# Two transformer blocks on one core: six weight chunks of the first block rounded and split by GpSimd, eight short vectors loaded later or not at all

## The chip, the cores and the metric

The kernel runs on one core of one Trainium2 chip. The metric is the device time of one launch in microseconds. The engines of the core are named as in the profile: PE (TensorE matmuls), PEld (its weight loads), DVE (VectorE), ACT (ScalarE), POOL (GpSimd) and SP (SyncE, which here only issues DMAs).

## The reference, cut to what matters

Two blocks run one after the other on 256 tokens of width 1024, in float32, each with two layers. The change touches the first block only, whose layer is:

```python
def hybrid_layer(x, c, positions, ...):
    mod = jax.nn.silu(c) @ w_ada + b_ada
    shift, scale, gate = jnp.split(mod[:, None, :], 3, axis=-1)
    h = rms_norm(x, norm_g) * (1 + scale) + shift
    z = h @ w_in
    c_q, c_kv, k_rope, g_mla, q_b, k_b, v_b, g_moba = jnp.split(z, list(IN_OFFSETS), axis=-1)
    o_mla = mla_attention(c_q, c_kv, k_rope, positions, mla_q_norm_g, mla_w_uq,
                          mla_kv_norm_g, mla_w_ukv, mla_q_g, mla_k_g)
    o_moba = moba_attention(q_b, k_b, v_b, moba_q_g, moba_k_g, rel_bias)
    y = jnp.concatenate([jax.nn.silu(g_mla) * o_mla, jax.nn.silu(g_moba) * o_moba], axis=-1) @ w_out
    return x + gate * y
```

With 256 tokens the "moba" attention is one causal block with a bias by distance. Its 8 heads have width 64; the "mla" attention has 8 heads of 96, whose last 32 columns are rotated. The second block (two SwiGLU feed-forwards around three attentions) needs four lambda vectors, a norm's gain and the sinks, the "short vectors" of the change.

## The kernel before

**Products.** Every matrix product keeps nearly full float32 accuracy with three passes. A weight chunk (128 partitions x 1024 or 512 columns) is loaded by SP into one of 6 buffers `raw`. ACT rounds it to fp32r into one of 5 buffers `wh` (line 903, signal `hi`), DVE subtracts to get the rest into `wl` (line 1513, signal `lo`), and PE multiplies x_h by wh, x_h by wl and x_l by wh (line 472). A chunk of 1024 columns gives PE 12 matmuls. ACT works up to four chunks ahead of PE and DVE three (class `Stream`, `take` and `split`), in a place of each engine's own program that is fixed when the kernel is built. A `wh` buffer is written again when PE has done the chunk five before it; SP issues the load of chunk c when chunk c - 6 has both `hi` and `lo`.

**Other loads in the same buffers.** The rows of `w_ada` also pass through `raw`. DVE adds each, weighed by silu(c), to a row (`weigh`; the profile names it by where the row lies: `acc`, `qt`, `qkv`, always `SCALAR_TENSOR_TENSOR x<-raw,st,x`).

**Order of a layer of the first block, `l` = 0 and 1.** PE runs the gemms z, qb, kb, vb (the last three give `qkv`), then turns the normed queries and keys (`turn_heads`, line 476), then the gemms q0, q1, kv0, kv1 (4 chunks: 1024, 512, 512 and 512 columns) and gmla (4 chunks of 1024). The moba attention runs as side steps between these gemms. One step k is: PE scores (`pb<-kt,qt`), DVE adds the bias and takes the maximum (line 1516), ACT takes the exponential (`pb<-pb,st`), PE turns the result, ACT copies it (`pt<-pb`), PE multiplies by v (`pb<-qkv,pt`). There are eight scores, k0 to k7. In the four steps of gmla the function `prep` is mixed in: ACT squares the mla queries (`th<-mq`), DVE sums them (line 2023), POOL takes the power -0.5 (`rstd`, line 2422), DVE waits for it before its next line-1516 operation. The evictions `qkv`, `mq`, `mkv` and the copies `qt`, `kt` are ACT's.

**POOL** has little work: the `rstd` of 1 or 8 columns, DMAs of broadcast rows, and 16 additions `G<-G,mg` of 512 columns in the second block (line 2504). After the `rstd` of qb of layer 0 it issues `vectors()` (line 2438): ten DMAs that broadcast short rows over all partitions into `bc`, 1424 columns in all.

Of the kernel before, what the change touches and what calls it, by code (L numbers as in the profile page):

```python
# [8 lines left out]
F = mybir.dt.float32  # L9
# [11 lines left out]
NRAW = 6  # L21
# [229 lines left out]
def build(nc, d, out, ctx):  # L251
# [16 lines left out]
    cols = sb("cols", [128, 128])  # L268
    bc = sb("bc", [128, 1440])
    st = sb("st", [128, NSTAT])  # L270
# [87 lines left out]
    bc_of, bc_in, n_bc = {}, [], 0  # L358
    for name, n in (("mla_q_g", 96), ("mla_k_g", 96), ("moba_q_g", 64), ("moba_k_g", 64),
                    ("diff_lambda_q1_2", 64), ("diff_lambda_k1_2", 64), ("diff_lambda_q2_2", 64),  # L360
                    ("diff_lambda_k2_2", 64), ("diff_subln_g_2", 128), ("sw_sink_2", 8)):
        bc_of[name] = (n_bc, n)
        bc_in.append((name, n_bc, NL * n))
        n_bc += NL * n
# [99 lines left out]
    def pe(e):  # L464
# [33 lines left out]
        def gemm(g, x, k0, key, src, n0, n, by, head=1, tail=1, between=None, mid=None, roll=0, soon=None,  # L498
                 two_sides=False):
            wv = src.rearrange("(c p) n -> p c n", p=128)  # L500
# [5 lines left out]
            pair_no[0] += 1  # L506
            first_bank = 2 * ((pair_no[0] - 1) % 2)
            for gi, group in enumerate(groups(nk, n, head, tail)):
                taken = [take(wv[:, (c0 + roll) % nk:(c0 + roll) % nk + kk, :, wide] if two_sides else
                              wv[:, (c0 + roll) % nk:(c0 + roll) % nk + kk, wide], kk, n,  # L510
                              ("mm", g, 1) if c0 + kk == nk else None) for c0, kk in group]
                for t in range(2):
                    o = banks[first_bank + t][:, 0:n]
                    for (c0, kk), (c, hi, lo) in zip(group, taken):
                        for k in range(kk):
                            kx, final = k0 + c0 + k, c0 + k == nk - 1
                            xh, xl = (v[:, kx, t * 128:t * 128 + 128] for v in x)
                            if c0 + k == 0:
                                open_bank(first_bank + t, (by, g, t))
                            w.wait_ge(*at("xh", *key(t, kx)))  # L520
                            w.wait_ge(*at("hi", c))
                            mm(o, xh, hi[:, k, :], c0 + k == 0, False)
                            w.wait_ge(*at("lo", c))
                            mm(o, xh, lo[:, k, :], False, False)
                            w.wait_ge(*at("xl", *key(t, kx)))
                            last = mm(o, xl, hi[:, k, :], False, final)
                            if final:
                                last.then_inc(*up("mm", g, t))
                            elif t == 1 and k == kk - 1:
# [166 lines left out]
        for l in range(NL):  # L696
# [49 lines left out]
            gemm(("kv0", l), XC, 2, ckey, d["mla_w_ukv"][l], 0, 512, "eva")  # L746
            gemm(("kv1", l), XC, 2, ckey, d["mla_w_ukv"][l], 512, 512, "eva")
            side.mix((None for _ in range(6)), 6)
            side.over(4)
            gemm(("gmla", l), XT, 0, xkey, win, 416, 512, "evd")  # L750
            side.drain()
# [138 lines left out]
    def act(e):  # L890
# [17 lines left out]
        def split(chunks):  # L908

            for c in chunks:  # L910
                src, kk, n, _, i, ada_ = plan[c]
                if ada_:
                    continue
# [580 lines left out]
    def dve(e):  # L1494
# [27 lines left out]
        def split(chunks):  # L1522

            for c in chunks:
                src, kk, n, _, i, ada_ = plan[c]
                if ada_:
                    weigh(c)
                    continue
                w.wait_ge(*at("hi", c))
                if i >= NW:  # L1530
# [313 lines left out]
        for l in range(NL):  # L1844
# [173 lines left out]
            def prep():  # L2018
                for t in range(2):
# [6 lines left out]
                    qr = heads(mq[:, t, :], 96)[:, :, 64:96]  # L2026
                    w.wait_ge(*at("bc"))
                    w.wait_ge(*at("eva", ("q1", l), t))
# [384 lines left out]
    def pool(e):  # L2413
# [20 lines left out]

        def vectors():

            for name, a0, n in bc_in:
                e.dma_start(bc[:, a0:a0 + n], bass.AP(tensor=d[name].tensor, offset=0, ap=[[0, 128], [1, n]])).then_inc(
                    *landed("bc"))

# [7 lines left out]
        for l in range(NL):  # L2448
# [36 lines left out]
        for l in range(NL):  # L2485
            for kind in ("f1", "mx", "f2"):
# [34 lines left out]
    def sp(e):  # L2521
        w = Waits(e)
        for c, (src, kk, n, _, _, _) in enumerate(plan):
            if c >= NRAW:
# [67 lines left out]
```

## Time and profile before

| | us |
|---|---|
| median of 3 runs | 1612.37 (1612.14 to 1613.6) |
| profiled execution, its own time | 1614.55 |
| its span, first to last instruction | 1612.7 |
| PE busy | 1561.8 |
| DVE, ACT, POOL busy | 1070.1, 872.2, 119.7 |
| mean granted TensorE clock | 0.992 of full speed |

PE is busy 97% of the span, so an engine other than PE matters only where PE waits for it or for what it delays. The stretches of the first attention are 80 to 132 us (layer 0) and 237 to 276 us (layer 1). Times on the left of a row are microseconds from the start of the span. A row of the waits or the timeline shows in brackets how long the engine stood idle before it, and what ended that.

### The profile page before, as it was taken

The page shows a single profiled execution, that of the slowest core. Times are in us where ns is not written, and L with a number is a line of the kernel's source. Part 1 is how long each engine was busy: PE and PEld are TensorE (multiplying, and loading weights), DVE is VectorE, ACT ScalarE, POOL GpSimd, SP SyncE. Part 2 cuts the span into 40 slices and gives each one's busy share as a digit, 9 for nine tenths or more (in the row PEclk, how much of TensorE's full clock was granted, in tenths as well). Part 3 has the DMA queues.
Part 4 walks back from the last instruction along what each step waited for, and adds up shares of the span by engine and source line. Part 5 has one row for each costly group of instructions (what it writes and reads, how often), then busy time and mean ns, then how long its engine had stood idle before and what let it go on. Part 6 is the DMA issues. An engine that isn't in the chain of part 4 may idle for free.

```text
span 1612.7 us, 21335 instructions
## 1 busy us (share of the span) xinstructions
PE 1561.8 (97%) x7540; PEld 1295.7 (80%) x7540; DVE 1070.1 (66%) x1779; ACT 872.2 (54%) x1526; POOL 119.7 (7%) x146
## 2 busy tenths in 40 slices
PE   5989999999999999999999999999999999999998
PEld 4768787788888888887788887888788888778886
DVE  7977877665555667687755647565666678676553
ACT  3676567554444656564644446444566656554442
POOL 0400021011000000021000001000000002100000
PEclk9999999999999999999999999999999999999999
DMA  9974473379855534546655557975553454665651
GB/s 341 303 252 157 161 253 122 101 183 220 212 183 169 183 93 137 176 144 209 195 183 183 190 189 190 194 205 195 170 183 112 143 158 145 202 207 171 200 185 73
DMA packets 149090, 293.16 MB, mean 182 GB/s; under 512 B 10128, under 2 KB 23216, under 8 KB 148984
## 3 DMA queue, kind: packets, MB, share of 16 engines
q1 hardware_dynamic: 143424, 276.60, 52.0%
q0 software_dynamic: 4416, 12.29, 6.9%
q10 hardware_dynamic: 1144, 2.92, 0.5%
q8 instruction: 60, 0.98, 0.2%
q14 instruction: 46, 0.38, 0.1%
HBM read 290.70 MB, written 1.06 MB: 181 GB/s over the span
## 4 chain that ended last, share of the span: by engine, by line
PE 86%; DVE 5%; ACT 4%; DMA 3%; issue 2%; POOL 1%; SPq 0%; DVEq 0%; POOLq 0%; ACTq 0%
PE pb L472 81%; PE pb L476 4%; DVE wl L1513 1%; DMA raw<-in_w_in 1%; DMA raw<-in_w_ada 1%; ACT wh L903 1%; DVE xt_l L1510 1%; DMA raw<-in_mla_w_ukv 1%; ACT pb L903 1%; DVE mkv L1510 1%; POOL st L2422 0%; DVE h L1510 0%; ACT xt_h L903 0%; ACT ti L903 0%; DVE st L2023 0%
## 5 line engine op out<-in xcount | busy, mean ns | idle before, releaser
L903 ACT ACTIVATE wh<-raw 128x1024 fp32r<-128x1024 f32 (+1 forms) x484 | 507.5, 1054 | 432.3 <-PE pb L472 408.0
L1513 DVE TENSOR_TENSOR wl<-raw,wh 128x1024 fp32r<-128x1024 f32 (+1 forms) x484 | 582.7, 1220 | 203.1 <-ACT wh L903 198.3
L472 PE MATMUL pb<-wh,xt_h 128*128 128x512 f32 (+2 forms) x1472 | 579.7, 394 | 5.4 <-issue 2.9
L472 PE MATMUL pb<-wh,xt_l 128*128 128x512 f32 (+2 forms) x1472 | 574.0, 390 | 2.8 <-DVE xt_l L1510 1.7
L472 PE MATMUL pb<-wl,xt_h 128*128 128x512 f32 (+2 forms) x1472 | 570.8, 388 | 0.0
L472 PEld LDWEIGHTS pb<-wh,xt_l 128*128 128x128 f32 x1472 | 277.8, 189 | 67.6 <-DVE xt_l L1510 10.2
L472 PEld LDWEIGHTS pb<-wh,xt_h 128*128 128x128 f32 x1472 | 278.3, 189 | 61.5 <-issue 7.2
L472 PEld LDWEIGHTS pb<-wl,xt_h 128*128 128x128 f32 x1472 | 278.4, 189 | 53.1
L472 PE MATMUL pb<-wh,big_h 128*128 128x512 f32 x352 | 137.8, 391 | 0.0
L472 PE MATMUL pb<-wh,big_l 128*128 128x512 f32 x352 | 137.1, 389 | 0.0
L472 PE MATMUL pb<-wl,big_h 128*128 128x512 f32 x352 | 136.9, 389 | 0.0
L2422 POOL TENSOR_TENSOR st<-st,cols 128x1 f32<-128x1 f32 (+2 forms) x56 | 54.7, 982 | 926.9 <-DVE st L1510 665.8
L472 PEld LDWEIGHTS pb<-wh,big_l 128*128 128x128 f32 x352 | 66.1, 188 | 13.9
L472 PEld LDWEIGHTS pb<-wl,big_h 128*128 128x128 f32 x352 | 66.1, 188 | 13.6
L472 PEld LDWEIGHTS pb<-wh,big_h 128*128 128x128 f32 x352 | 66.1, 188 | 13.4
L1510 DVE SCALAR_TENSOR_TENSOR sgt<-ti,pb 128x512 f32<-128x512 f32 (+1 forms) x48 | 30.7, 644 | 61.2 <-ACT ti L903 61.0
L1510 DVE SCALAR_TENSOR_TENSOR hid<-pb,few,sgt 128x512 f32<-128x512 f32 (+1 forms) x48 | 33.9, 706 | 47.2 <-PE pb L472 46.3
L903 ACT ACTIVATE p<-p,st 128x256 f32<-128x256 f32 x96 | 48.3, 504 | 29.4 <-DVE st L1516 29.4
L903 ACT ACTIVATE pt<-pb 128x512 f32<-128x512 f32 (+1 forms) x80 | 40.3, 504 | 26.3 <-PE pb L476 26.3
L903 ACT ACTIVATE big_h<-pb 128x512 fp32r<-128x512 f32 x44 | 24.2, 597 | 39.1 <-PE pb L476 39.1
L903 ACT ACTIVATE ti<-pb,few 128x512 f32<-128x512 f32 (+1 forms) x48 | 31.4, 657 | 20.8 <-PE pb L472 20.3
L2504 POOL TENSOR_TENSOR G<-G,mg 128x512 f32<-128x512 f32 x16 | 24.3, 1522 | 246.2 <-DVE mg L1510 245.8
(243 smaller groups left out, 1552.6 us busy)
## 6 DMA issues: line engine op xcount, KB each, us to landing
raw<-in_ffn_w_gu SPq DMA_DIRECT2D x160, 512.0 KB, 4.7
raw<-in_w_in SPq DMA_DIRECT2D x148, 512.0 KB, 4.2
raw<-in_ffn_w_down SPq DMA_DIRECT2D x88, 512.0 KB, 4.0
raw<-in_w_ada SPq DMA_DIRECT2D x48, 512.0 KB, 5.4
raw<-in_w_out SPq DMA_DIRECT2D x32, 512.0 KB, 4.2
raw<-in_w_branch SPq DMA_DIRECT2D x24, 512.0 KB, 4.0
raw<-in_ffn_w_gu SPq DMA_DIRECT2D x32, 256.0 KB, 4.9
raw<-in_w_in SPq DMA_DIRECT2D x8, 416.0 KB, 4.6
```

The costliest lines, as they stand in the source:

```text
L472: return e.matmul(o, a, b, start=start, stop=stop)
L476: return e.transpose(o, a, ident[0:n, 0:n])
L903: return e.activation(o, a, func, **kw)
L1510: return e.scalar_tensor_tensor(out=o, in0=a, scalar=s, in1=b, op0=op0, op1=op1)
L1513: return e.tensor_tensor(o, a, b, op)
L2422: e.tensor_tensor(stat(n, "rs", *name), v, halves.to_broadcast([128, n]) if n > 1 else halves, ALU.pow).then_inc(*up("rs", *name))
L2504: e.tensor_tensor(m, m, mg[mg_at(n, n0, t)][:, :], ALU.add).then_inc(*up("mrg", g, t))
```

## The change

- `gemm` gets an argument `pool`, a set of chunk numbers. In each layer chunk 0 of kv1 (512 columns) and chunks 1 and 3 of gmla (1024 columns each) are marked. ACT and DVE leave them out; POOL makes both parts in a new function `split`: `tensor_copy` for wh (signal `hip`), then `tensor_tensor` subtract for wl (`lop`). PE and SP wait for `hip` and `lop` where they waited for `hi` and `lo`.
- In POOL's program kv1's chunk and gmla's chunk 1 come before the `rstd` of the first half of the mla queries, gmla's chunk 3 between that and the next `rstd`.
- `vectors` at its old place issues only the two mla gains (384 columns, signal `bcm`). The two moba gains, read by nothing from `bc`, are dropped (256 columns). The six vectors of the second block (784 columns) are issued in the first feed-forward of the second block.

```diff
-            gemm(("kv1", l), XC, 2, ckey, d["mla_w_ukv"][l], 512, 512, "eva")
+            gemm(("kv1", l), XC, 2, ckey, d["mla_w_ukv"][l], 512, 512, "eva", pool=(0,))
...
-            gemm(("gmla", l), XT, 0, xkey, win, 416, 512, "evd")
+            gemm(("gmla", l), XT, 0, xkey, win, 416, 512, "evd", pool=(1, 3))
...
+        def split(g, *which):
+
+            for c0 in which:
+                c = pool_splits[g, c0]
+                kk, n, _, i, _ = plan[c][1:6]
+                hi, lo, v = (a[i % m][:, 0:kk * n] if m == NW else a[c % m][:, 0:kk * n]
+                             for a, m in ((wh, NW), (wl, NW), (raw, NRAW)))
+                w.wait_ge(*at(f"raw{c % NRAW}", c))
+                if i >= NW:
+                    w.wait_ge(*at(*plan[split_at[i - NW]][3]))
+                e.tensor_copy(hi, v).then_inc(*up("hip", c))
+                w.wait_ge(*at("hip", c))
+                e.tensor_tensor(lo, v, hi.bitcast(F), ALU.subtract).then_inc(*up("lop", c))
...
                 if l == 0 and nm == "qb":
-                    vectors()
-            for nm in ("mq", "mk"):
-                for t in range(2):
-                    rstd(8, nm, l, t)
+                    vectors(bc_in[:2], "bcm")
+            split(("kv1", l), 0)
+            split(("gmla", l), 1)
+            rstd(8, "mq", l, 0)
+            split(("gmla", l), 3)
+            for nm, t in (("mq", 1), ("mk", 0), ("mk", 1)):
+                rstd(8, nm, l, t)
...
                     if kind == "f1":
+                        if l == 0:
+                            vectors(bc_in[2:], "bc")
                         bias_table(s, l)
```

POOL in layer 0, from the power for qb on. Before:

```order
16 L2422 TENSOR_TENSOR st<-st,cols 128x8 [waits s_var] x2
17 L2438 DMA bc<-in_mla_q_g 128x192
18 L2438 DMA bc<-in_mla_k_g 128x192
19 L2438 DMA bc<-in_moba_q_g 128x128
20 L2438 DMA bc<-in_moba_k_g 128x128
21 L2438 DMA bc<-in_diff_lambda_q_2 128x128
22 L2438 DMA bc<-in_diff_lambda_k_2 128x128
...
25 L2438 DMA bc<-in_diff_subln_g 128x256
26 L2438 DMA bc<-in_sw_sink 128x16
27 L2422 TENSOR_TENSOR st<-st,cols 128x8 [waits s_var] x6
28 L2470 DMA mk<-in_b_ada 128x1024 [waits s_tr]
```

The same place after the change (`CAST` is the `tensor_copy`; 128x512 is kv1's chunk, the 128x1024 ones are gmla's):

```order
16 L2438 TENSOR_TENSOR st<-st,cols 128x8 [waits s_var] x2
17 L2454 DMA bc<-in_mla_q_g 128x192
18 L2454 DMA bc<-in_mla_k_g 128x192
19 L2438 TENSOR_TENSOR st<-st,cols 128x8 [waits s_var] x2
20 L2467 CAST wh<-raw 128x512 [waits s_w,s_raw3]
21 L2469 TENSOR_TENSOR wl<-raw,wh 128x512 [waits s_hip]
22 L2467 CAST wh<-raw 128x1024 [waits s_mm,s_raw1]
23 L2469 TENSOR_TENSOR wl<-raw,wh 128x1024 [waits s_hip]
24 L2438 TENSOR_TENSOR st<-st,cols 128x8 [waits s_var]
25 L2467 CAST wh<-raw 128x1024 [waits s_mm,s_raw0]
26 L2469 TENSOR_TENSOR wl<-raw,wh 128x1024 [waits s_hip]
27 L2438 TENSOR_TENSOR st<-st,cols 128x8 [waits s_var] x3
```

The eight other DMAs are gone from here, and the powers of the mla queries (rows 24 and the first of 27) now stand behind the splits.

ACT in layer 0, from the rounding of q0's chunk on. Before:

```order
68 L903 ACTIVATE wh<-raw 128x1024 [waits s_raw4]
69 L903 ACTIVATE wh<-raw 128x512 [waits s_w,s_raw0]
70 L903 ACTIVATE wh<-raw 128x512 [waits s_w,s_raw1]
71 L903 ACTIVATE wh<-raw 128x512 [waits s_w,s_raw3]
72 L903 ACTIVATE qkv<-pb 128x512 [waits s_mm] x2
73 L903 ACTIVATE qt<-pb 128x512 [waits s_tr] x2
```

After:

```order
68 L917 ACTIVATE wh<-raw 128x1024 [waits s_raw4]
69 L917 ACTIVATE wh<-raw 128x512 [waits s_w,s_raw0]
70 L917 ACTIVATE wh<-raw 128x512 [waits s_w,s_raw1]
71 L917 ACTIVATE qkv<-pb 128x512 [waits s_mm] x2
72 L917 ACTIVATE qt<-pb 128x512 [waits s_tr] x2
```

The rounding of kv1's chunk (row 71 before) no longer stands ahead of the evictions of vb and the copies `qt`.

DVE in layer 1, around the first score. Before:

```order
319 L1513 TENSOR_TENSOR wl<-raw,wh 128x512 [waits s_raw4,s_w,s_hi]
320 L1510 SCALAR_TENSOR_TENSOR acc<-raw,st,acc 128x1024 [waits s_acc,s_raw5]
321 L1513 TENSOR_TENSOR wl<-raw,wh 128x512 [waits s_raw0,s_w,s_hi]
322 L1516 ISA pb,st<-pb,mbias 128x128 [waits s_pt,s_sc]
...
326 L1513 TENSOR_TENSOR wl<-raw,wh 128x1024 [waits s_raw1,s_mm,s_hi]
327 L1510 SCALAR_TENSOR_TENSOR acc<-raw,st,acc 128x1024 [waits s_acc,s_raw2]
```

After:

```order
316 L1527 TENSOR_TENSOR wl<-raw,wh 128x512 [waits s_raw4,s_w,s_hi]
317 L1524 SCALAR_TENSOR_TENSOR acc<-raw,st,acc 128x1024 [waits s_acc,s_raw5]
318 L1530 ISA pb,st<-pb,mbias 128x128 [waits s_pt,s_sc]
...
322 L1527 TENSOR_TENSOR wl<-raw,wh 128x1024 [waits s_raw1,s_mm,s_hi]
323 L1524 SCALAR_TENSOR_TENSOR acc<-raw,st,acc 128x1024 [waits s_acc,s_raw2]
324 L1530 ISA pb,st<-pb,mbias 128x128 [waits s_pt,s_sc]
```

Only the subtraction of kv1's chunk (row 321 before) left this place; the split of gmla's chunk 0 (row 322 after) and a weighed row still stand between the first score and the second.

## Rows read from the trace of the kernel before

**Rows 1.** The page's chain that ended last, share of the span by engine.

```profile
PE 86%; DVE 5%; ACT 4%; DMA 3%; issue 2%; POOL 1%; SPq 0%; DVEq 0%; POOLq 0%; ACTq 0%
```

**Rows 2.** PE's waits from 60 to 335 us: total, times, longest.

```profile
PE pb L472 <- ACT pt L903: 5.2, 5, 1.5
PE pb L476 <- ACT qt L903: 3.8, 1, 3.8
```

**Rows 3.** Timeline of ACT, layer 0: start, duration, operation, [idle before].

```profile
85.16 0.63 ACT L903 ACTIVATE wh<-raw 128x512 fp32r<-128x512 f32 x1 [1.32 <-DMA raw<-in_mla_w_ukv]
85.69 1.07 ACT L903 ACTIVATE qkv<-pb 128x512 f32<-128x512 f32 x2
...
101.57 1.07 ACT L903 ACTIVATE wh<-raw 128x1024 fp32r<-128x1024 f32 x1
```

**Rows 4.** DMA from 70 to 80 us: queue, packets, MB, share of 16 engines.

```profile
q0 software_dynamic: 332, 0.66, 71.3%
q1 hardware_dynamic: 445, 0.73, 24.4%
```

**Rows 5.** Timeline of PE, layer 0.

```profile
82.92 0.55 PE L476 MATMUL pb<-cst,qkv 128*128 128x128 f32 x3 [0.21 <-DVE qkv L1513]
87.30 1.11 PE L476 MATMUL pb<-cst,qkv 128*128 128x128 f32 x4 [3.83 <-ACT qt L903]
88.07 0.77 PE L472 MATMUL pb<-wh,xc_h 128*128 128x512 f32 x1
...
122.25 1.97 PE L472 MATMUL pb<-qkv,pt 128*128 128x64 f32 x8 [1.50 <-ACT pt L903]
```

**Rows 6.** Timeline of DVE, layer 0, the end of the gemm vb.

```profile
78.78 2.28 DVE L1513 TENSOR_TENSOR mbias<-sg,cst 128x2048 f32<-128x2048 f32 x1
80.99 0.68 DVE L1513 TENSOR_TENSOR wl<-raw,wh 128x512 fp32r<-128x512 f32 x1
81.59 1.28 DVE L1513 TENSOR_TENSOR qkv<-qkv,st 128x512 f32<-128x512 f32 x2
```

**Rows 7.** Stretches of PE: us, PE busy, granted clock, DMA share, GB/s.

```profile
85.00:91.00 6.00, 3.70 (x11) 0.50 0.97 343
122.00:129.00 7.00, 6.75 (x20) 0.51 0.38 111
269.00:272.00 3.00, 3.00 (x10) 0.50 0.22 72
```

**Rows 8.** POOL's groups by shape: busy, mean ns of one | idle before.

```profile
L2504 POOL TENSOR_TENSOR G<-G,mg 128x512 f32<-128x512 f32 x16 | 24.3, 1522 | 246.2 <-DVE mg L1510 245.8
L2441 POOL MEMSET ones<- 128x128 f32 x1 | 0.2, 205 | 0.3 <-POOLq L2577 0.3
```

**Rows 9.** POOL and DVE from 738 to 743 us, single operations, ns min/median/max.

```profile
L2504 POOL TENSOR_TENSOR G<-G,mg x2: 1293/1747/2201, 738.7 to 740.1; 128x512 f32<-128x512 f32 x2
L1513 DVE TENSOR_TENSOR wl<-raw,wh x2: 1221/1768/2314, 739.9 to 741.1; 128x1024 fp32r<-128x1024 f32 x2
```

**Rows 10.** Timeline of DVE, layer 1, from the first score to the second.

```profile
241.25 1.22 DVE L1513 TENSOR_TENSOR wl<-raw,wh 128x1024 fp32r<-128x1024 f32 x1
242.39 1.28 DVE L1510 SCALAR_TENSOR_TENSOR acc<-raw,st,acc 128x1024 f32<-128x1024 f32 x1
243.58 0.28 DVE L1516 CUSTOM_DVE_ANT_0 pb<-pb,mbias 128x128 f32<-128x128 f32 x1
```

**Rows 11.** Timeline of PE, layer 1.

```profile
244.94 0.41 PE L476 MATMUL pb<-cst,pb 128*128 128x128 f32 x2 [0.19 <-ACT pb L903]
...
251.02 1.13 PE L472 MATMUL pb<-kt,qt 128*128 128x512 f32 x2 [1.21 <-ACT pt L903]
...
268.34 1.50 PE L472 MATMUL pb<-qkv,pt 128*128 128x64 f32 x8 [1.51 <-ACT pt L903]
```

**Rows 12.** The chain that ended last, layer 1: start, us, what.

```profile
256.44 1.75 POOL st L2422
...
262.59 1.75 POOL st L2422
```

**Rows 13.** Timeline of DVE, layer 1, between these two powers.

```profile
259.87 1.22 DVE L1513 TENSOR_TENSOR wl<-raw,wh 128x1024 fp32r<-128x1024 f32 x1
261.30 1.01 DVE L2023 TENSOR_REDUCE st<-th 128x4 f32<-128x384 f32 x2 [0.21 <-ACT th L903]
```

More of the change, by code:

```diff
@@ L268, in build @@
     cols = sb("cols", [128, 128])
-    bc = sb("bc", [128, 1440])
+    bc = sb("bc", [128, 1184])
     st = sb("st", [128, NSTAT])
@@ L358, in build @@
     bc_of, bc_in, n_bc = {}, [], 0
-    for name, n in (("mla_q_g", 96), ("mla_k_g", 96), ("moba_q_g", 64), ("moba_k_g", 64),
-                    ("diff_lambda_q1_2", 64), ("diff_lambda_k1_2", 64), ("diff_lambda_q2_2", 64),
+    for name, n in (("mla_q_g", 96), ("mla_k_g", 96), ("diff_lambda_q1_2", 64), ("diff_lambda_k1_2", 64), ("diff_lambda_q2_2", 64),
                     ("diff_lambda_k2_2", 64), ("diff_subln_g_2", 128), ("sw_sink_2", 8)):
@@ L395, in chunk_view, with upper, lower @@
         return buf[:, 0:kk * n].rearrange("p (k n) -> p k n", n=n)
+    pool_splits = {}
+    def upper(c):
+        return ("hip" if c in pool_splits.values() else "hi", c)
+    def lower(c):
+        return ("lop" if c in pool_splits.values() else "lo", c)
     def weighed(l, j, kx):
@@ L498, in gemm @@
         def gemm(g, x, k0, key, src, n0, n, by, head=1, tail=1, between=None, mid=None, roll=0, soon=None,
-                 two_sides=False):
+                 two_sides=False, pool=()):
             wv = src.rearrange("(c p) n -> p c n", p=128)
@@ L507, in gemm @@
             first_bank = 2 * ((pair_no[0] - 1) % 2)
+            n_chunk = 0
             for gi, group in enumerate(groups(nk, n, head, tail)):
+                for i in range(len(group)):
+                    if n_chunk in pool:
+                        pool_splits[g, n_chunk] = c_no[0] + i
+                    n_chunk += 1
                 taken = [take(wv[:, (c0 + roll) % nk:(c0 + roll) % nk + kk, :, wide] if two_sides else
@@ L520, in gemm @@
                             w.wait_ge(*at("xh", *key(t, kx)))
-                            w.wait_ge(*at("hi", c))
+                            w.wait_ge(*at(*upper(c)))
                             mm(o, xh, hi[:, k, :], c0 + k == 0, False)
-                            w.wait_ge(*at("lo", c))
+                            w.wait_ge(*at(*lower(c)))
                             mm(o, xh, lo[:, k, :], False, False)
@@ L911, in split @@
                 src, kk, n, _, i, ada_ = plan[c]
-                if ada_:
+                if ada_ or c in pool_splits.values():
                     continue
@@ L1528, in split @@
                     continue
+                if c in pool_splits.values():
+                    continue
                 w.wait_ge(*at("hi", c))
@@ L2026, in prep @@
                     qr = heads(mq[:, t, :], 96)[:, :, 64:96]
-                    w.wait_ge(*at("bc"))
+                    w.wait_ge(*at("bcm"))
                     w.wait_ge(*at("eva", ("q1", l), t))
@@ L2433, in bcast, with vectors @@
                         ).then_inc(*landed(f"ring{i}", *key))
-        def vectors():
-            for name, a0, n in bc_in:
+        def vectors(which, to):
+            for name, a0, n in which:
                 e.dma_start(bc[:, a0:a0 + n], bass.AP(tensor=d[name].tensor, offset=0, ap=[[0, 128], [1, n]])).then_inc(
-                    *landed("bc"))
+                    *landed(to))
+        def split(g, *which):
[10 more added lines that the diff above has]
+                e.tensor_tensor(lo, v, hi.bitcast(F), ALU.subtract).then_inc(*up("lop", c))
         e.memset(ones[:, :], 1.0).then_inc(*up("ones"))
@@ L2528, in sp @@
                 else:
-                    w.wait_ge(*at("hi", c - NRAW))
-                    w.wait_ge(*at("lo", c - NRAW))
+                    w.wait_ge(*at(*upper(c - NRAW)))
+                    w.wait_ge(*at(*lower(c - NRAW)))
             if len(src.shape) == 4:
```

## The prediction

> **What bounds the kernel now.** I read the page's chain first: 86% of the path to the end is PE [rows 1]. So only PE's waits in the two stretches that change are at stake. In the list of PE's waits from 60 to 335 us two releasers carry almost everything: the `pt` copies of ACT, 5.2 us in five waits, and one wait of 3.8 us for `qt` [rows 2]. The timelines say why each happens.
>
> The 3.8 us lie at 87.30 us in layer 0 [rows 5]. ACT could not evict vb and copy `qt` because the rounding of kv1's chunk stands ahead of them in its program and its data had not landed; it ran at 85.16 us [rows 3]. The data was late because from 70 to 80 us POOL's queue, which is the broadcast of `vectors()`, held the DMA engines for 71.3% of the time, with 0.66 MB, and the weights' queue for 24.4% [rows 4]. The `pt` waits are the tail of a long chain: DVE's subtraction of a chunk and a weighed row stand between the first and the second score's maximum [rows 10], and later the mla queries' powers stand twice on the chain, 1.75 us each [rows 12], with DVE's work around them [rows 13]. Three stretches run at 0.50 of the clock (1.2 GHz instead of 2.4) after PE stood idle for 3.83, 1.50 and 1.51 us [rows 5, 7, 11].
>
> **What the change costs on POOL.** The trace has no split on POOL. The subtraction is nearest to POOL's 128x512 addition, 1.29 us undisturbed [rows 9], so 1.29 for kv1's chunk and 2.58 for one of gmla. For the rounding of 1024 columns the floor is ACT's own 1.07 us [rows 3], the ceiling the 2.58 us of an operation with two inputs; eight times the memset of 128 columns (0.205 us) gives 1.64 with its start counted eight times [rows 8]. I take 1.1, nearest to the memset without its starts, and 0.5 for kv1's. The mean of the addition in rows 8, 1.52 us, is above 1.29 because some were held up, and that is the point on which this prediction turns.
>
> **Layer 0, start of q0.** Without the eight broadcasts (1040 of 1424 columns, about 5 of those 7.1 us of DMA time) and with kv1's rounding gone from ACT, the 3.83 us wait falls. Next late is DVE: the normed keys are ready at 82.87 (81.59 + 1.28) [rows 6], PE turns four blocks by 83.5, four more in 0.6, and q0 starts at 84.2 instead of 88.07. But POOL is free at about 79 us, kv1's data should be there, and DVE is in the 2.28 us `mbias` until 81.06 [rows 6]. Then they alternate: rounding to 81.55, DVE's subtraction to 82.15, POOL's to 83.35, DVE's norms (1.2) to 84.55, PE's turns 1.15, q0 at 85.7. **Gain 2.3 us** of the possible 3.9. The clock falls here as before, because PE still stands idle for over 3 us.
>
> **Layer 0, scores.** POOL starts gmla's chunk 1 when q0 is done, and DVE meets it in the same two instructions as in rows 10. The weighed row behind the subtraction is held up about 2.6 us. Against that, ACT loses two roundings of 0.95 us each (1.07 less overlap, [rows 3]). At the last score but two: 2.3 + 1.9 - 2.6 = 1.6 us ahead. The subtraction of chunk 3 leaves DVE, worth 0.6 (ACT's squares are next late): 2.2 ahead at the first power. Then POOL takes chunk 3: rounding 1.1, subtraction 2.58, while DVE wants to subtract a chunk of gmoba. That costs 1.8 (worked out below for layer 1), leaving **0.4 us**. The second idle stretch of PE begins some 2 us earlier, so the slow clock until 129 us [rows 7] may end earlier; half speed gives back at most 1 us of that, I take 0.5. Layer 0: **-0.9 us**.
>
> **Layer 1, first scores.** Here ACT waits for no DMA and nothing is gained at q0. POOL starts chunk 1 when q0 is done, at 240.4, and rounds to 241.5. DVE's subtraction (241.25, 1.22) ends 242.65 instead of 242.4; POOL's then runs to 245.1; the weighed row (242.39, 1.28), with two SBUF inputs, is held until then and ends at 246.1. The maximum of the second score stands behind it and moves from 243.58 to 246.1, **2.5 us** later, and PE's turn from 244.94 to 247.4 [rows 10, 11]. ACT's rounding of chunk 3 (0.95) is gone from the path behind it, so the score at 251.02, which waited 1.21 for ACT [rows 11], comes at 252.5: 1.5 later. PE stands idle for 2.7 us in between, and idle times of 1.5 us were followed by the slow clock [rows 7, 11]. Its matmuls up to that score would take twice as long where they were partly hidden by ACT: nothing to 2 us; I take 0.5. Now **+2.0 us**.
>
> **Layer 1, powers.** The first power (256.44 + 1.75, [rows 12]) still comes first. POOL then rounds for 1.1 and subtracts to 261.8 (old clock of events). DVE's subtraction at 259.87 [rows 13] is held for 1.8 to 1.9 us; 0.21 of it was spent waiting anyway: **+1.6 us**. The second power (262.59) moves by as much, and with it the last score, the copies and PE's matmuls at 268.34. POOL is free just in time for it, 0.7 us before it is wanted, so it is not queued behind the split. Layer 1: **+3.6 us**.
>
> **What stays hidden.** PE wants the POOL chunks 5 us or more after they are ready. SP's loads behind a buffer that POOL frees up to 9 us later are gmoba's last chunk, weighed rows and `w_out`, needed later still. The six broadcasts in the feed-forward (784 columns, some 4 us of DMA time) meet PE with four chunks (11 us) rounded ahead. Their use comes 200 us later.
>
> **Sum:** -0.9 + 3.6 = **+2.7 us** on the profiled execution of 1614.55 us (span 1612.7). The median of the runs is 1612.37, so I forecast **1615.1 us**. A difference under 0.2% (3.2 us) is about what a measurement of this kernel can't tell from no change.
>
> The Trainium skill (GPSIMD Engine Reference, performance versus the Vector engine) gives 4497 ns for an addition of 2048 columns, so an estimate of 2.25 us for 1024; with it each of the four large subtractions holds DVE 0.33 less and the sum would be +1.4. The rows' 1.29 for 512 decides here.
>
> **Rivals.** (a) *POOL doesn't hold DVE*, because its waiting instruction loses to DVE's next one, or the loads land between. Then layer 0 gains 3.9, 1.3 from a clock that doesn't fall there, 0.8 at the fifth score and 0.6 at the power, 6.6; layer 1 gains 0.95 and 0.2. That is -7.8: **1604.6 us**. Rows 9 speak against it, twice; rows 4 for its first term. Chance 0.16. (b) *Only kv1's split misses DVE's norms*, because its data lands after 81.6 us or DVE runs ahead: 1.6 to 2.4 more gain in layer 0, about **1613.0**. Chance 0.16. (c) *The rounding is slow*, 2.58 us like an operation with two inputs. It decides from about 1.8 us on: then POOL's subtractions end after the second power is wanted and the power queues behind them. Cost: 0.6 at q0, 1.4 in each chunk 1 of layer 1, 1.5 at the powers: +3.5, **1618.6 us**, slower. Chance 0.18. (d) *The broadcasts starve the feed-forward*, or a split comes late for PE: +3 or more, chance 0.06. (e) *The change does nothing* that reaches PE: 1612.4, chance 0.04. The forecast itself has 0.40, with 1612.5 to 1617.5 as its own range, since each slow-clock term can turn out 0 or 2.
>
> **How the numbers follow.** Faster by over 0.2%: (a) and a part of (b), 0.20. Within: (e), most of (b), some 0.26 of the forecast's 0.40: 0.43. Slower: (c), (d) and the rest, 0.37. The range leaves out the far part of (a) and of (d): 1606 to 1618.8.
>
> **What would show it.** Right: in the changed trace DVE subtractions and weighed rows of up to 3.7 us next to POOL's; the 3.83 us wait gone and q0 at 85.7; in layer 1 PE idle for over 2 us before the turn at 247.4, and the second power 3.6 later. Wrong: DVE's durations unchanged there; a POOL rounding well over 1.1 us; q0 at 84.2; PE waits in the feed-forward.

## The result and the profile after

| | us | ratio to before |
|---|---|---|
| before, median of 20 runs | 1612.8 (1611.0 to 1614.0) | |
| after, median of 20 runs | 1614.36 (1612.6 to 1622.7) | 1.0016 [1.0010, 1.0023] |
| after, profiled execution | 1613.96, span 1612.1 | |

The changed kernel is slower by 0.16% (2.6 us by the ratio, 1.6 by the medians): a real difference, and within what the forecast called the same. The forecast was +2.7 us. Four of the twenty runs of after took more than 1617 us; none of before did. In the three slowest (1619.7 to 1622.7 us) the mean granted clock was 0.986 to 0.989, in the others 0.991 to 0.995. Ratios here and below leave out the executions that were far above all others (8930 us, once, of before; 3165 us, once, in e3).

The answers to [rows 1] and [rows 2]: the chain's shares, and PE's waits from 60 to 335 us (total, times, longest).

```profile
PE 85%; DVE 7%; issue 4%; DMA 2%; ACT 2%; POOL 1%; DVEq 0%; SPq 0%; POOLq 0%; ACTq 0%
```

```profile
PE pb L485 <- ACT pb L917: 6.8, 4, 2.5
PE pb L481 <- ACT pt L917: 3.0, 2, 1.5
PE pb L485 <- DVE qkv L1527: 1.7, 2, 1.5
```

The 3.8 us for `qt` are gone and the waits for `pt` are down from 5.2 to 3.0, but a releaser that had stood for 1.1 us, ACT's exponential `pb`, now stands for 6.8. What was gained at one end was paid at the other.

**Layer 0.** PE's timeline, against [rows 5]:

```profile
82.94 0.98 PE L485 MATMUL pb<-cst,qkv 128*128 128x128 f32 x7 [0.21 <-DVE qkv L1527]
83.68 0.47 PE L481 MATMUL pb<-wh,xc_h 128*128 128x512 f32 x1
...
115.81 0.66 PE L485 MATMUL pb<-cst,pb 128*128 128x128 f32 x4 [1.69 <-ACT pb L917]
117.97 1.47 PE L481 MATMUL pb<-qkv,pt 128*128 128x64 f32 x8 [1.50 <-ACT pt L917]
```

q0 starts at 83.68, 4.4 us earlier than before and 2.0 earlier than forecast. ACT copies `qt` at 80.62 instead of after 85.69. Two things are new there: ACT no longer rounds kv1's chunk, and the DMA engines from 70 to 80 us are free for the weights [rows 3, 4]. e1 and e2 below take them apart.

```profile
80.62 1.08 ACT L917 ACTIVATE qt<-pb 128x512 f32<-128x512 f32 x2
```

```profile
q1 hardware_dynamic: 898, 1.99, 64.2%
q0 software_dynamic: 88, 0.17, 5.2%
```

POOL's queue fell from 71.3% to 5.2% of the engines' time, and the weights' queue moved 1.99 MB in place of 0.73. Now POOL and DVE there [rows 6]:

```profile
79.01 6.14 POOL L2467 CAST wh<-raw 128x512 fp32r<-128x512 f32 x1
85.23 2.15 POOL L2469 TENSOR_TENSOR wl<-raw,wh 128x512 fp32r<-128x512 f32 x1
```

```profile
78.80 2.28 DVE L1527 TENSOR_TENSOR mbias<-sg,cst 128x2048 f32<-128x2048 f32 x1
81.00 0.68 DVE L1527 TENSOR_TENSOR wl<-raw,wh 128x512 fp32r<-128x512 f32 x1
81.61 1.28 DVE L1527 TENSOR_TENSOR qkv<-qkv,st 128x512 f32<-128x512 f32 x2
82.81 0.68 DVE L1527 TENSOR_TENSOR wl<-raw,wh 128x512 fp32r<-128x512 f32 x1
...
84.78 1.45 DVE L1524 SCALAR_TENSOR_TENSOR acc<-raw,st,acc 128x1024 f32<-128x1024 f32 x1
```

The rounding of 512 columns stood on POOL for 6.14 us, where layer 1's takes 0.69, and ended 0.4 us into DVE's weighed row of 84.78, which took 1.45 instead of 1.28. The norms at 81.61 took their normal 1.28. It was POOL that waited here, not DVE. Between 83.41 and 84.78 DVE ran another weighed row, of 1.27 us; it ended at 84.68. So there are 0.1 us between it and the next one, the first break in DVE's work since 78.8. The rounding ends 0.5 us behind it, so this is most likely where POOL got its turn.

The granted clock in stretches of after. The columns are: us; busy time and count of PE, PEld, DVE, ACT and POOL; granted clock; DMA share; GB/s.

```profile
85.00:91.00 6.00, 4.73 (x28) 3.70 (x26) 5.08 (x10) 5.62 (x12) 4.75 (x4) 1.00 0.91 294
...
119.00:122.00 3.00, 3.00 (x10) 2.42 (x10) 2.83 (x10) 1.08 (x2) 1.58 (x2) 0.51 0.43 124
122.00:129.00 7.00, 6.76 (x51) 5.88 (x50) 6.97 (x12) 5.20 (x10) 0.51 (x2) 1.00 0.53 174
```

PE was idle for under 1.5 us at a time before q0, and ran at full clock (2.4 GHz) from 85 to 91 us, where before it was at half. Half clock came from 119 to 122 us, around the idle 1.50 us of 117.97; from 122 to 129 us the clock was full, where [rows 7] has 0.51.

**Layer 1.** DVE, POOL and PE around the second score, against [rows 10, 11]:

```profile
235.98 1.36 DVE L1527 TENSOR_TENSOR wl<-raw,wh 128x1024 fp32r<-128x1024 f32 x1
237.26 3.40 DVE L1524 SCALAR_TENSOR_TENSOR acc<-raw,st,acc 128x1024 f32<-128x1024 f32 x1
240.59 0.28 DVE L1530 CUSTOM_DVE_ANT_0 pb<-pb,mbias 128x128 f32<-128x128 f32 x1
```

```profile
236.34 3.24 POOL L2469 TENSOR_TENSOR wl<-raw,wh 128x1024 fp32r<-128x1024 f32 x1
```

```profile
241.93 0.66 PE L485 MATMUL pb<-cst,pb 128*128 128x128 f32 x2 [2.47 <-ACT pb L917]
265.45 0.66 PE L485 MATMUL pb<-cst,pb 128*128 128x128 f32 x4 [1.33 <-ACT pb L917]
```

The turns are taken as forecast: POOL's subtraction (2.38 us when alone) waits 0.9 for DVE's; the weighed row waits for POOL's and takes 3.40 instead of 1.28; with the 0.14 by which DVE's own subtraction is longer, PE is 2.3 us later behind the maximum, and is idle for 2.47 us (the 1.33 us of 265.45 are taken up under "Layer 1, powers" below). Then the clock falls (columns as above):

```profile
242.00:244.00 2.00, 2.00 (x9) 1.81 (x9) 0.52 (x5) 2.00 (x7) 0.00 (x0) 0.50 0.88 309
```

How far PE is ahead of before, read from the starts of the same matmuls in both timelines:

| in before at | 88.07 | 105.28 | 120.09 | 133.78 | 196.36 | 236.04 | 244.94 | 249.03 | 251.02 | 266.18 | 278 to the end |
|---|---|---|---|---|---|---|---|---|---|---|---|
| after earlier by | 4.4 | 5.8 | 4.3 | 5.6 | 5.1 | 5.3 | 3.0 | 0.5 | 1.9 | 0.7 | 0.7 to 1.0 |

### The profile page after: what moved, and what is told of

It is laid out like the page before. It is cut to its first block, busy times and chain, and to the rows that moved or that the text cites. A ratio compares the mean times of both kernels' runs of the same rounds, so it can differ in the third digit from the quotient of the medians.

```text
span 1612.1 us, 21331 instructions
## 1 busy us (share of the span) xinstructions
PE 1561.1 (97%) x7540; PEld 1296.1 (80%) x7540; DVE 1070.0 (66%) x1773; ACT 865.7 (54%) x1520; POOL 144.6 (9%) x156
## 4 chain that ended last, share of the span: by engine, by line
PE 85%; DVE 7%; issue 4%; DMA 2%; ACT 2%; POOL 1%; DVEq 0%; SPq 0%; POOLq 0%; ACTq 0%
PE pb L481 81%; PE pb L485 4%; DVE wl L1527 2%; DMA raw<-in_w_ada 1%; DVE xt_l L1524 1%; DMA raw<-in_w_in 1%; DVE mkv L1524 1%; POOL st L2438 0%; DVE h L1524 0%; POOL wl L2469 0%; DVE qt L1524 0%; ACT ti L917 0%; ACT wh L917 0%; ACT xt_h L917 0%; DVE pb L1530 0%
## 5 line engine op out<-in xcount | busy, mean ns | idle before, releaser
L917 ACT ACTIVATE wh<-raw 128x1024 fp32r<-128x1024 f32 (+1 forms) x478 | 500.8, 1054 | 425.0 <-PE pb L481 395.8
L917 ACT ACTIVATE pb<-pb,st 128x128 f32<-128x128 f32 (+1 forms) x64 | 28.6, 449 | 28.6 <-DVE st L1530 28.0
```

The source lines that it names most:

```text
L917: return e.activation(o, a, func, **kw)
```

## The experiments

Ratios are to the kernel before, run on the same chip alongside; half an interval is 0.0009 to 0.0015, or 1.5 to 2.4 us. Three chips were used: one for e1 to e4, one for e5 to e8, one for e9 to e12. e5 has no row: of its two runs one took 2297 us.

| kernel | median us | ratio [95%] |
|---|---|---|
| the change, again (e7) | 1613.99 | 1.0011 [1.0001, 1.0020] |
| before, again (e6) | 1612.41 | 0.9996 [0.9986, 1.0006] |
| e1 vectors only | 1607.76 | 0.9977 [0.9968, 0.9986] |
| e2 splits only | 1619.96 | 1.0045 [1.0030, 1.0061] |
| e3 small copy at the start | 1621.86 | 1.0064 [1.0052, 1.0076] |
| e4 splits in layer 0 only | 1609.73 | 0.9988 [0.9978, 0.9998] |
| e8 only kv1's splits | 1609.65 | 0.9982 [0.9973, 0.9991] |
| e9 chunk 1 of layer 1 later | 1611.91 | 1.0000 [0.9991, 1.0009] |
| e10 two splits, layer 1 | 1608.29 | 0.9979 [0.9970, 0.9988] |
| e11 kv1's split after `mbias` | 1614.39 | 1.0022 [1.0013, 1.0031] |
| e12 unused tile | 1622.39 | 1.0070 [1.0057, 1.0084] |

### e1 and e2: the two halves of the change apart

e1 (all splits back on ACT and DVE):

```diff
-            gemm(("kv1", l), XC, 2, ckey, d["mla_w_ukv"][l], 512, 512, "eva", pool=(0,))
+            gemm(("kv1", l), XC, 2, ckey, d["mla_w_ukv"][l], 512, 512, "eva")
...
-            gemm(("gmla", l), XT, 0, xkey, win, 416, 512, "evd", pool=(1, 3))
+            gemm(("gmla", l), XT, 0, xkey, win, 416, 512, "evd")
...
-            split(("kv1", l), 0)
-            split(("gmla", l), 1)
...
-            split(("gmla", l), 3)
```

> The short vectors as in the changed kernel, but no chunk on GpSimd. Theory V (layer 0's gain comes from the broadcasts that are gone from 70 to 80 us, and the splits bring only layer 1's loss): the 3.8 us wait of PE for qt is gone, q0 starts at 83.7 to 84.5 instead of 88.07, no slow clock from 85 to 91 us, PE some 4 to 5 us ahead at 133 us and still so at 275 us; in all 4 to 5 us faster than before (ratio 0.997). Rival S (ACT had to lose the rounding of kv1's chunk for this): the wait for qt stays at 2 us or more and the gain is under 2 us.

Measured: 3.7 us faster by the ratio, 4.0 by the medians, where 4 to 5 were expected. ACT's rounding of kv1's chunk stands ahead of the evictions as before, but its data is there; then PE:

```profile
77.92 0.63 ACT L917 ACTIVATE wh<-raw 128x512 fp32r<-128x512 f32 x1 [1.21 <-DMA raw<-in_mla_w_ukv]
```

```profile
83.62 0.48 PE L481 MATMUL pb<-wh,xc_h 128*128 128x512 f32 x1
...
238.16 0.41 PE L485 MATMUL pb<-cst,pb 128*128 128x128 f32 x2 [0.20 <-ACT pb L917]
241.28 1.13 PE L481 MATMUL pb<-kt,qt 128*128 128x512 f32 x2 [0.20 <-ACT pt L917]
244.24 1.12 PE L481 MATMUL pb<-kt,qt 128*128 128x512 f32 x2 [1.21 <-ACT pt L917]
```

Theory V holds and rival S falls: q0 starts at the same moment as in the changed kernel. Moving the loads is enough for all of the gain at q0, and none of it needs POOL. The first row also settles that kv1's data was there at 77.92, before POOL was free for it at 79.01.

e2 (three splits per layer as changed, ten broadcasts at the old place; the tile `bc` has its old 1440 columns again, not shown):

```diff
                     vectors(bc_in[:2], "bcm")
+                    vectors(bc_in[2:], "bc")
...
-                        if l == 0:
-                            vectors(bc_in[2:], "bc")
```

> The three splits per layer on GpSimd, the vectors all loaded at their old place (ten broadcasts). Theory V alone: the broadcasts still fill the DMA engines, so most of the 3.8 us stays somewhere (PE waits for a chunk instead of qt) and layer 1 loses 4.4 us: 3 to 4 us slower than before. If ACT's place behind kv1's data was enough (rival S): q0 starts near 84 all the same, layer 0 gains 4 to 5 us, layer 1 loses 4.4: within 1 us of before.

Measured: 7.3 us slower by the ratio, more than either expectation said. Two of the seven runs took 1614.1 us, the other five 1619.4 to 1622.4; the profiled one (1621.2) is of the longer kind. Three views of it: POOL, DVE, PE.

```profile
84.97 1.08 POOL L2468 CAST wh<-raw 128x512 fp32r<-128x512 f32 x1 [5.70 <-DMA raw<-in_mla_w_ukv]
```

```profile
92.32 3.36 DVE L1525 SCALAR_TENSOR_TENSOR acc<-raw,st,acc 128x1024 f32<-128x1024 f32 x1
```

```profile
85.15 0.68 PE L486 MATMUL pb<-cst,qkv 128*128 128x128 f32 x4 [1.45 <-ACT qt L918]
85.56 0.70 PE L482 MATMUL pb<-wh,xc_h 128*128 128x512 f32 x1
...
96.16 1.87 PE L482 MATMUL pb<-ones,qt 128*128 128x1 f32 x8 [2.20 <-DVE st L1531]
97.89 0.77 PE L482 MATMUL pb<-wh,xc_h 128*128 128x512 f32 x1
```

With kv1's rounding off ACT, q0 starts 2.5 us earlier than before in spite of the late data (the wait for `qt` is 1.45 us), so at q0 the splits alone bring 2.5 us and the loads alone 4.4. But chunk 1's split now meets the weighed row of layer 0 in full (3.36 us), PE waits 2.20 us, and its matmuls of 512 columns take 0.63 us instead of 0.39 until 102 us: half clock. Neither expectation had this in layer 0; layer 1 lost what it loses in the changed kernel (4.7 us from 236 to 278 us of before).

### e4 and e8: where the splits cost

e4 calls `split` only for `l == 0`; e8 only for kv1's chunk, in both layers.

```diff
-            split(("kv1", l), 0)
-            split(("gmla", l), 1)
+            if l == 0:
+                split(("kv1", l), 0)
+                split(("gmla", l), 1)
             rstd(8, "mq", l, 0)
-            split(("gmla", l), 3)
+            if l == 0:
+                split(("gmla", l), 3)
```

> The changed kernel, but GpSimd splits only in layer 0; layer 1 as before. Theory (layer 0 gained 5.2 us, layer 1 lost 4.4): PE 5 us ahead at 240 us and still 5 at 275, the weighed row behind the subtraction back at 1.28 us, no wait of 2.5 us for pb, 4 to 5 us faster than before. If layer 1's loss came from elsewhere (the clock, the moved vectors), it stays: within 1 us of before.

> The changed kernel with only kv1's chunk on GpSimd; the gmla chunks back to ACT and DVE in both layers. Theory (the chunks of 1024 columns cost, by holding up a weighed row for 0.8 to 2.1 us and a subtraction for 0.9, kv1's costs nothing): as e1, 4 us faster than before, the weighed row in layer 1 back at 1.28 us. Rival (kv1's split costs as well, by the norms or by its late end): 1 to 3 us slower than e1.

Measured: e4 1.9 us faster than before, e8 2.9. By differences of ratios, from e1 on: the splits of layer 0 cost 1.8 us, those of layer 1 another 4.5 (3.7 if e7's ratio stands for the change), and together they turn e1's -3.7 into the change's +2.6 (+1.8). The 1.8 us of layer 0 are hardly more than half an interval and rest mainly on the traces. kv1's two splits cost 0.8 us, which the intervals don't tell from nothing. In e4, layer 1's turn is back at a wait of 0.21 (first row); in e8 the wait of 1.69 us that the changed kernel has at 115.81 is 0.22 (second row), so that one belongs to a chunk of gmla in layer 0. It is chunk 3, which POOL splits from 105.86 to 109.35 us: between 105.28 and 120.09 us of before, PE loses 1.5 us in after, in e4 and in e7, and none in e1 and in e8.

```profile
239.90 0.41 PE L485 MATMUL pb<-cst,pb 128*128 128x128 f32 x2 [0.21 <-ACT pb L917]
```

```profile
115.05 0.66 PE L485 MATMUL pb<-cst,pb 128*128 128x128 f32 x4 [0.22 <-ACT pb L917]
```

e4 gained 2 to 3 us less than was expected from the trace of before. About 2 us of that are the yardstick's fault, as the next run shows.

### e6 and e7: both kernels profiled again

> The kernel before, for a second profile: the one at hand took 1614.55 us, its runs without a profile 1611.8 to 1612.8. If the wait of PE for qt varies with the DMA, it is under 3.8 us here and the profiled time nearer 1612; if the profile itself costs 2 us, it is 1614 again with the same waits.

> The changed kernel once more, for the spread of its runs (1612.6 to 1622.7, three of twenty over 1617). Theory (two levels, by whether PE's idle stretches are followed by half clock): times near 1613 to 1615 and some near 1620 to 1622. The profile shows kv1's rounding at 79 us for 6 us again and q0 at 83.7 when it is one of the first kind.

Before, again: PE's wait for `qt` is again 3.8 us, and the wait at 121.87 is 1.50 as in [rows 5], but from 122 to 129 us the clock is full, where [rows 7] has 0.51:

```profile
122.00:129.00 7.00, 6.68 (x45) 5.69 (x45) 6.77 (x16) 5.07 (x11) 2.72 (x2) 1.00 0.40 127
```

So an idle stretch of 1.50 us is followed by half clock in one execution and not in the next. PE was 1.7 us later at 133.78 in the first profile of before, 1.3 of it from this stretch; the profiled execution of e6 took 1612.6 us instead of 1614.55. After, again, took 1614.99 us: kv1's rounding 6.14 us, q0 at 83.65, the weighed row 3.40, all the same, and half clock in a different set of stretches. Against e6, the change gains 3.9 us (first profile) or 2.6 (second) up to 133.78 us of before, and loses 4.6 in layer 1 (236 to 278 us), in both.

### e9: the same work, begun later

```diff
+            if l == 1:
+                w.wait_ge(*at("top", "moba", 1, 1, 1))
             split(("gmla", l), 1)
```

`top` is DVE's signal for the maximum of the second score.

> The changed kernel with one more wait: in layer 1 GpSimd begins gmla's chunk 1 only after DVE's maximum of the second score (the third instruction behind the subtraction). The same work on every engine. Theory L (the 3.2 us that PE loses up to 251 us come from the weighed row held up by the split, and from the half clock after that): the weighed row takes 1.28 us, PE's wait of 2.5 us for pb is gone, and with it the half clock from 242 to 248; ACT's freed rounding is kept. 3 to 4 us faster than the changed kernel, 1.5 to 2.5 us faster than before. Rival (the loss comes from the load on SBUF or from the chunk's late end): within 1 us of the changed kernel.

DVE, then PE:

```profile
237.14 1.28 DVE L1524 SCALAR_TENSOR_TENSOR acc<-raw,st,acc 128x1024 f32<-128x1024 f32 x1
...
241.57 1.94 DVE L1527 TENSOR_TENSOR wl<-raw,wh 128x1024 fp32r<-128x1024 f32 x1 [0.45 <-ACT wh L917]
```

```profile
239.69 0.41 PE L485 MATMUL pb<-cst,pb 128*128 128x128 f32 x2 [0.19 <-ACT pb L917]
242.81 1.13 PE L481 MATMUL pb<-kt,qt 128*128 128x512 f32 x2 [0.20 <-ACT pt L917]
244.82 1.12 PE L481 MATMUL pb<-kt,qt 128*128 128x512 f32 x2 [0.26 <-ACT pt L917]
```

Theory L holds: with every instruction still there, and only the start of chunk 1's split moved, the weighed row is back at 1.28 us, the wait of 2.47 at 0.19, no half clock follows it, and PE is 4.3 us ahead of the changed kernel at 251 us of before. A subtraction of DVE that nobody waits for is held up instead (1.94). The last row is the freed rounding: 0.26 us of wait in place of 1.21. The size was less than expected in the runs: 1.8 to 2.6 us faster than the changed kernel by the ratios (3 to 4 expected), level with before (1.5 to 2.5 faster expected). The profiled execution (1609.8) was one of the quickest of eleven (1609.6 to 1614.1).

### e10: the cheapest two splits

Layer 1 only, kv1's chunk and gmla's chunk 1, the latter after the same wait; no chunk 3.

```diff
+            if l == 1:
+                split(("kv1", l), 0)
+                w.wait_ge(*at("top", "moba", 1, 1, 1))
+                split(("gmla", l), 1)
```

> The vectors as changed, and on GpSimd only kv1's chunk and gmla's chunk 1 of layer 1, the latter after DVE's maximum of the second score; gmla's chunk 3 and all of layer 0 stay with ACT and DVE. Theory L: nothing of DVE's chain is held up, ACT has a rounding less (PE's wait of 1.2 us for pt at 251 us shrinks): 0 to 1 us faster than e1, 4 to 5 us faster than before. Rival (any split on GpSimd next to the scores costs time): 1 to 3 us slower than e1.

```profile
244.27 1.12 PE L481 MATMUL pb<-kt,qt 128*128 128x512 f32 x2 [1.21 <-ACT pt L917]
```

Measured 0.9979, as e1 (0.9977), where 0 to 1 us more was expected. Nothing is lost and nothing gained: PE's starts in this stretch are those of e1 to 0.03 us. The 1.21 us wait stays, so it is chunk 3's rounding alone that stands on this path. e1 stays the simplest version that beats both kernels; the splits add nothing to it.

### e3, e5 and e11: why GpSimd waited six microseconds at 79 us

e3 adds a copy of 8 columns to fp32r at the start, into a tile of its own; e5 is the same kernel.

```diff
     bc = sb("bc", [128, 1184])
+    warm = sb("warm", [128, 8], R)
...
+        w.wait_ge(*at("ones"))
+        e.tensor_copy(warm[:, :], ones[:, 0:8])
```

> The changed kernel with one more tensor_copy on GpSimd, of 8 columns float32 to fp32r, at the start of the program. In the changed kernel the first one takes 6.14 us (79.01 to 85.15) where that of layer 1 takes 0.69. Theory C (the first of its kind costs GpSimd about 4 to 5 us once): the early small one takes 4 to 5 us, kv1's of layer 0 under 2.5 us, DVE's norms at 81.6 are then held up by it and by the subtraction, q0 starts at 85 to 86 instead of 83.7: 1 to 2 us slower than the changed kernel. Rival A (GpSimd lost its turn to DVE five times in a row): the early one takes 0.1 to 0.3 us, kv1's still 6 us, no change in time.

> The kernel of e3 once more, for a profile in the state of its other runs (1621.4 to 1623.3, some 7 us over the changed kernel; its only profile was of an execution of 3165 us). The early copy took 0.19 us there, so no first-time cost. Theory T (GpSimd's turn at 79 us decides): kv1's rounding gets its turn sooner than after 6 us, the norms of DVE are held up, q0 starts at 85 us or later, and more stretches run at half clock. Rival: 79 us looks as in the changed kernel and the 7 us are lost elsewhere, by the clock.

```profile
1.00 0.19 POOL L2475 CAST warm<-ones 128x8 fp32r<-128x8 f32 x1
```

The first copy of its kind took 0.19 us, and in e2 the first one took 1.08, so theory C (a cost of the first use) falls. The rest of e3 can't be read this way: both profiled executions were far off (3165 and 2297 us, PE slow throughout; in e5 POOL began kv1's rounding only at 104.80 us, and it took 0.72), and the other six runs of the two, 1621.4 to 1623.4 us, have another cause (e12). e5's own question, whether 79 us looks as in the changed kernel, is answered by e12, whose tiles lie as e3's:

```profile
78.67 6.14 POOL L2468 CAST wh<-raw 128x512 fp32r<-128x512 f32 x1
```

e11 lets POOL ask only when `mbias` is done:

```diff
+            w.wait_ge(*at("mbias"))
             split(("kv1", l), 0)
```

> The changed kernel with one more wait: GpSimd begins kv1's chunk of layer 0 only when DVE has done mbias (81.0 us), so that its request no longer falls into that instruction of 2.28 us; five more DVE instructions without a gap follow, as before. Theory M (GpSimd lost its turn because of where its request fell): the rounding now takes its turn behind DVE's next one, the norms are held up, q0 starts at 85 to 86 instead of 83.7, as forecast: 1 to 3 us slower than the changed kernel. Rival N (in a chain of DVE instructions of 512 columns that follow without a gap GpSimd gets no turn): the rounding again ends at 85.1 us, q0 at 83.7, no change.

```profile
80.96 4.02 POOL L2467 CAST wh<-raw 128x512 fp32r<-128x512 f32 x1 [2.09 <-DVE mbias L1527]
```

```profile
83.50 0.47 PE L481 MATMUL pb<-wh,xc_h 128*128 128x512 f32 x1
```

Asked 2 us later, it was served at the same point, in the same weighed row, and q0 did not move. Theory M falls. Rival N fits: while DVE went through a subtraction, two norms and a subtraction of 512 columns and a weighed row without a gap, POOL got no turn. It doesn't say why: behind a subtraction of 1024 columns POOL got its turn every time (236.34, 88.47 and [rows 9]), also without a gap. The order (ACT and DVE rows of the change above) has a wait for `s_acc` ahead of each weighed row, and two of them in a row start 1.37 to 1.39 us apart where the first takes 1.27 or 1.28, with or without POOL at work (83.41 in after, 101.12 and 101.49 in the two traces of before). Whether this gap, the size or the kind of instruction decides it was not tried and stays open.

### e12: the tile alone

e12 has e3's tile and not its copy.

> The changed kernel with the tile of 8 columns that e3 writes, declared and not used: all tiles behind it lie 32 bytes further in SBUF, and no instruction is added. Theory (the copy at the start causes e3's 7 us): no change against the changed kernel, 1613 to 1616 us. Rival (where the tiles lie does it): 1621 us as e3.

Measured 1.0070: 1622.39 us, 8 us over the changed kernel, so the place of the tiles does it; e3's copy isn't needed for it. All tiles behind `bc` lie 32 bytes further. PE's groups by shape, of e7 and then of e12:

```profile
L481 PE MATMUL pb<-wh,big_h 128*128 128x512 f32 x352 | 137.7, 391 | 0.0
```

```profile
L482 PE MATMUL pb<-wh,big_h 128*128 128x512 f32 x352 | 139.9, 398 | 0.0
```

A matmul that reads `big_h` takes 398 ns instead of 391, and `big_l` 395 instead of 389. Over 1056 such matmuls the busy time grew by 6.5 us, and over the 288 that read `xb_h` or `xb_l` by 1.2, together most of the 8. Those that read `xt_h`, which lies ahead of `bc`, are unchanged (396 in both). The change itself moves the same tiles, by 1024 bytes, since `bc` has 1184 columns in place of 1440. That costs nothing here: the means for `big_h` are 391 in before, in after, and in e2, which has the old width.

## Why the prediction came out right, step by step

The total was right (+2.7 forecast, +2.6 by the ratio, +1.8 in e7, +1.6 by the medians), and the turns in layer 1 were right as a mechanism. That it fits to 0.1 us is luck. Layer 0 gained 1.7 to 3.0 us more than forecast, layer 1 lost 1.0 more, and without the four long runs the mean of after is only 1.2 us over that of before; no trace shows one of those.

- **What bounded the kernel, and the cause of the 3.8 us wait: right.** e1 shows it directly: with only the loads moved, POOL's queue holds the DMA engines for 5.0% of 70 to 80 us and the weights' queue for 64.5%, and the wait is gone.
- **"Then they alternate ... q0 at 85.7": wrong.** The step that failed is the rule drawn from [rows 9], that "a waiting POOL comes before DVE's next instruction". It was drawn from one pair of 1024-column subtractions and carried to a gapless chain of other ones (81.00 to 83.41: two subtractions of 512 columns, two norms, a weighed row), where POOL was passed over five times, and four in e11. Measured: q0 at 83.68, the full 4.4 us, and the clock, said to fall there as before, stayed at full. Of the signs that the prediction named, q0 near 84.2 (wrong) is what came, not 85.7 (right). Rival (b) had the outcome in this place (kv1's split missing the norms); of its reasons, late data is ruled out by e1's 77.92. Rival (a) had named what happened here, that POOL's waiting instruction loses to DVE's next one, but for the whole kernel.
- **Layer 0's scores: right in kind.** "Held up about 2.6 us" was 0.8 (2.06 us at 88.72) and 0.4 (1.67 at 92.42), and stayed behind waits that e1 has too. Chunk 3's cost was forecast at 1.8 and is 1.5 in the traces (5.8 to 4.3 ahead in the table). All three splits together make layer 0's gain 5.6 in after, where e1 has 6.7. Layer 0 came to -2.6 to -3.9 us against e6 where -0.9 was forecast.
- **The yardstick:** the profile of before held a half-clock stretch (122 to 129 us) that e6 doesn't. It took 1614.55 us at a mean clock of 0.992; e6's eight runs took 1611.1 to 1612.7 at 0.993 to 0.996, so most runs probably don't hold it either. The forecast took 0.5 back from it. Adding the sum to the median of the runs, not to the profiled time, kept this out of the total.
- **Layer 1, first scores: right, a little short.** The maximum was forecast 2.5 us late and was 2.3; PE's wait forecast over 2 and measured 2.47. The term for the clock, 0.5, was the mis-sized one: PE lost 2.5 us more at half clock (3.0 ahead to 0.5). The freed rounding and what it hid gave back 1.4 where 0.95 was said. At 251.02: +3.4 (5.3 ahead to 1.9) against +2.0 forecast.
- **Layer 1, powers: right in sum.** Chunk 3's split held DVE twice, not once: the rounding of 256.15 held a scaling of 8 columns, which takes 0.17 in before and in e1, and POOL's subtraction held DVE's, which takes 1.22 in [rows 13]. Together that is 1.7 us of holding (1.8 to 1.9 forecast, all of it on the subtraction); the second power came 7.5 us behind the first instead of 6.2, and PE, idle for 1.33 us at 265.45, lost 1.2 where 1.6 was forecast. The same two lines stand in layer 0 (0.98 at 105.94, 2.08 at 108.36). Layer 1 in all: 4.6 against 3.6. Before, then after:

```profile
258.22 0.17 DVE L1507 TENSOR_SCALAR st<-st 128x8 f32<-128x8 f32 x1
```

```profile
256.24 0.98 DVE L1521 TENSOR_SCALAR st<-st 128x8 f32<-128x8 f32 x1
...
258.65 2.08 DVE L1527 TENSOR_TENSOR wl<-raw,wh 128x1024 fp32r<-128x1024 f32 x1
```

- **POOL's own costs: right.** The rounding of 1024 columns takes 1.04 us (1.1 taken), of 512 0.69 (0.5), the subtraction 2.38 and 1.29 (2.58 and 1.29). Rival (c) is out. The row of after by shape (one of the four, of 1.23 us, waited for DVE):

```profile
L2467 POOL CAST wh<-raw 128x1024 fp32r<-128x1024 f32 x4 | 4.3, 1085 | 6.4 <-PE pb L481 5.3 <-DMA raw<-in_w_in 1.1
```

- **The feed-forward: right.** After stays 0.7 to 1.0 us ahead from 278 us to the end, through the six broadcasts. Rival (d) is out.
- **The Trainium skill's rule** (SBUF — State Buffer, the shared port pair): the page states that one instruction holds the pair for its whole length and the other waits. It doesn't state that a waiting GpSimd comes before DVE's next instruction; that half of the prediction's rule came from [rows 9] alone, and it is the half that failed. On the whole-instruction hold layer 1 agrees, and for the one-input rounding layer 0 does (in after the weighed row at 88.72 took 2.06 us and waited 0.8 of it beside the rounding of 88.47). By the page the one that starts first gets the pair; at 79 us POOL had asked 2 us before DVE's subtraction of 81.00 and came five instructions later. The Trainium skill's figure of 4497 ns for an addition of 2048 columns (GPSIMD Engine Reference, performance versus the Vector engine) gives an estimate of 2.25 us for 1024; the runs show 2.38 for the subtraction.

Rival (a), 1604.6, was wrong on its premise in layer 1, where POOL held DVE for 2.12 us. e1, 1607.8, shows what the loads alone bring when nothing on POOL can disturb DVE.

## What to carry to other kernels

Work given to an idle GpSimd isn't free when VectorE is near the path: ask which VectorE instruction stands next to it and who waits for that one. If there is slack, place it by a wait behind the critical instruction: in e9 the same work, a few microseconds later, cost 1.8 to 2.6 us less. When a change has two parts, price them apart: here the broadcasts' move was worth 3.7 us and the splits, which looked like the point of the change, ate 5.5 to 6.3.

## What the runs showed of the hardware beyond this

- A GpSimd rounding of 512 columns (0.69 us alone) waited 5.4 us while VectorE ran instructions with SBUF inputs without a gap, and 3.3 us when it asked 2 us later (e11); both times it ended 0.5 us behind VectorE's first gap, of 0.1 us. GpSimd's roundings and subtractions that asked during a 1024-column subtraction had their turn behind it at once (88.47 and 236.34 in after).
- A GpSimd rounding of 1024 columns held a VectorE scaling of only 8 columns for 0.8 us (0.98 instead of 0.17), in after, e2, e7 and e9 alike; in e1, e4 and e8, without it, layer 1's scaling takes 0.17.
- With tiles 32 bytes further in SBUF, the matmuls that read them were 2% slower (391 to 398 ns each) and the kernel 8 us slower; 1024 bytes further made no difference (391 in before and in after). Whoever adds a small tile should compare these means before blaming what the tile is for, as e3 nearly did.
- The same idle stretch of PE of 1.50 us was followed by half clock (0.51) in one execution of before and by full clock in another.
